# A prompt chunk's end rearranged: the second norm and two query blocks by tiles of 128 tokens, eight expert names ranked ahead of the other eight

## The reference, cut to what matters

```python
h2 = modulate(rmsnorm(x1, g_norm2), sh2, sc2)          # xn * (1 + sc2) + sh2
x2 = x1 + gt2 * peer(h2, w_pq, sub_keys, u_tab, v_tab)

def peer(h, w_pq, sub_keys, u_tab, v_tab):             # 8 heads, 128 keys a side, 16384 experts
    q = (hf @ w_pq).reshape(n, 8, 2, 128)
    s = einsum('nhsd,hskd->nhsk', q, sub_keys)
    sv, si = top_k(s, 16)                              # 16 best keys of each half
    cand = sv[:, :, 0, :, None] + sv[:, :, 1, None, :] # 256 sums
    cidx = si[:, :, 0, :, None] * 128 + si[:, :, 1, None, :]
    fv, fp = top_k(cand, 16)                           # 16 of 256 sums: 16 experts
    eidx, g = take(cidx, fp), softmax(fv)
    u, vr = u_tab[eidx], v_tab[eidx]                   # one row of 1024 numbers per token and expert
    return sum((g * gelu(h . u)) * vr)
```

## Time and profile before

| what | value |
|---|---|
| median of 3 runs | 1992.36 us (1988.22 to 1995.3) |
| the profiled execution | 1991.84 us, span 1989.4 us |
| PE busy | 1354.3 us (68%) |
| DVE busy | 1252.0 us (63%) |
| POOL busy | 1094.6 us (55%) |
| ACT busy | 589.5 us (30%) |
| DMA | 701.83 MB, mean 353 GB/s; 545.33 MB of them by the gathers |
| first gather of `u_tab` starts at | 382.5 us |

### The profile page before, as it was taken

How to read it: one execution, slowest core, us unless ns; L and a number is a source line. 1 busy time by engine, 2 the same in 40 slices (tenths; PEclk the granted TensorE clock), 3 DMA queues, 4 the chain that set the end, 5 groups by cost and what they waited for, 6 DMA issues and landing times.

```text
span 1989.4 us, 23567 instructions
## 1 busy us (share of the span) xinstructions
PE 1354.3 (68%) x7318; PEld 873.8 (44%) x7318; DVE 1252.0 (63%) x3037; ACT 589.5 (30%) x1653; POOL 1094.6 (55%) x1062
## 2 busy tenths in 40 slices
PE   6998999857879677988878777444443444544344
PEld 5887799745646445666655544111110111111111
DVE  3265436477788888866667756656667666666640
ACT  2446424233245245222223323112112212211110
POOL 0100000256665556765666767777777777677774
PEclk9999999978989889889989888556566666765667
DMA  9755346699999988999999999999999999999997
GB/s 366 261 176 206 108 159 200 217 382 370 396 349 407 343 324 328 385 409 370 408 407 409 409 407 396 400 409 404 403 407 401 408 403 402 381 409 408 390 402 292
DMA packets 202443, 701.83 MB, mean 353 GB/s; under 512 B 22568, under 2 KB 32368, under 8 KB 202032
## 3 DMA queue, kind: packets, MB, share of 16 engines
q0 software_dynamic: 149760, 545.33, 70.0%
q1 hardware_dynamic: 52560, 155.02, 21.3%
HBM read 691.26 MB, written 11.06 MB: 353 GB/s over the span
## 4 chain that ended last, share of the span: by engine, by line
DMA 20%; issue 14%; POOL 14%; PE 8%; DVE 3%; POOLq 0%; ACT 0%; DVEq 0%; ACTq 0%
DMA arena<-in_v_tab,pku 14%; POOL arena L2153 14%; DMA arena<-in_u_tab,pku 6%; PE y L1149 5%; PE acc L796 2%; DVE arena L1990 1%; PE acc L936 1%; POOLq L2149 0%; DVE pku L2011 0%; PE acc L833 0%; DVE pk L2010 0%; PE turned L1132 0%; DVE pku L2027 0%; DVE arena L1611 0%; DVE pk L2026 0%
## 5 line engine op out<-in xcount | busy, mean ns | idle before, releaser
L1149 PE MATMUL y<-arena 128*32 128x512 f32 x2080 | 413.8, 909 | 495.9 <-DMA arena<-in_v_tab,pku 495.8
L2153 POOL DMA_INDIRECT arena<-in_u_tab,pku x520 | 551.7, 1061 | 344.9 <-issue 156.3
L2153 POOL DMA_INDIRECT arena<-in_v_tab,pku x520 | 527.9, 1015 | 294.0 <-issue 149.1
L796 PE MATMUL acc<-arena 128*128 128x264 f32 (+1 forms) x2304 | 547.4, 395 | 17.4 <-ACT arena L1259 7.8
L796 PEld LDWEIGHTS acc<-arena 128*128 128x128 f32 x2304 | 445.4, 196 | 122.5 <-issue 49.7
L1990 DVE CUSTOM_DVE_ANT_0 arena<-arena,h_bank 128x1024 f32<-128x1024 f32 x240 | 290.8, 1218 | 254.1 <-DMA arena<-in_u_tab,pku 253.3
L1149 PEld LDWEIGHTS y<-arena 128*32 128x32 f32 x2080 | 81.8, 143 | 728.2 <-issue 723.5
L1990 DVE CUSTOM_DVE_ANT_0 arena<-arena 128x1024 f32<-128x1024 f32 x280 | 335.2, 1221 | 84.7 <-DMA arena<-in_u_tab,pku 72.4
L1486 ACT ACTIVATE pk<-pk 128x1 f32<-128x1 f32 x520 | 103.5, 281 | 2.1
L1504 ACT CAST pku<-turned 128x8 uint32<-128x8 f32 x64 | 10.3, 160 | 293.6 <-PE turned L1133 293.6
L1132 PE MATMUL turned<-arena 128*128 128x256 f32 x128 | 58.2, 545 | 55.5 <-DVE arena L2068 55.4
(11 more groups left out here) (249 smaller groups left out, 1873.5 us busy)
## 6 DMA issues: line engine op xcount, KB each, us to landing
arena<-w_mod SPq DMA_DIRECT2D x48, 512.0 KB, 6.2
arena<-w_pq SPq DMA_DIRECT2D x32, 512.0 KB, 7.1
arena<-w_xr SPq DMA_DIRECT2D x20, 512.0 KB, 9.0
arena<-w_qk SPq DMA_DIRECT2D x20, 512.0 KB, 7.0
arena<-w_gr SPq DMA_DIRECT2D x20, 512.0 KB, 6.5
arena<-w_rnn SPq DMA_DIRECT2D x16, 640.0 KB, 7.1
arena<-in_u_tab,pku POOLq DMA_INDIRECT x520, 8.0
arena<-in_v_tab,pku POOLq DMA_INDIRECT x520, 7.8
```

Of the source, the lines that this page charges most:

```text
L796: mm = pe.matmul(a[:, 0:n], w[:, k, :], rhs[:, k, 0:n], start=(k == 0), stop=(k == ks - 1))
L1149: mm = pe.matmul(y[rows, h, :], spread[g % NTURN][:, 32 * j:32 * j + 32], rows_v[j][:, h * 512:(h + 1) * 512], start=first and (g != SAMPL ...
L2153: pool.indirect_dma_start(out=row, out_offset=None, in_=table, in_offset=bass.IndirectOffsetOnAxis(ap=idx, axis=0), **more).then_inc(signa ...
```

## The change

The products of chunk 0 behind `norm` 1 are put in another order and two of them are cut in half. Behind the norm come `pqa` 0 and 1 (query blocks 0 and 1 for the first 128 tokens), `first`, `pqb` 0 and 1 (the same blocks for the other 128 tokens), then `mod` 10, `mod` 11, `modT` 10, `modT` 11, then `rowsx` 0 to 3, then `pq` 2 and on as before. h2 is made tile by tile: DVE multiplies by the gain (`scale_tiles`), ACT adds the shift (`shift_rows`). A new function `first_names` on DVE finds the eight best names of head 0 from the 64 sums of the 8 best keys of each side and writes them itself; POOL's first gather waits for it (`s_first`). The other eight names come as before, from 16 keys of each side and 256 sums, out of `best_keys`, `best_sums`, `experts` and `number`. ACT runs `spread_keys`, the copies up to `rowsx` 2, `number` and `exponentials` in this order. The weights of `pq` 0, `pq` 1 and `keys` 0 take the ring's places ahead of those of `mod` 10 and 11, and `pq` 2 and 3 are loaded when `pqb` 0 and 1 are done.

```diff
+        "gains": [("mod", 10), ("mod", 11), ("modT", 10), ("modT", 11)]}
...
         product(ch, "norm", 1, (), 3.5)
-        mods(ch, "norm")
+        if ch == 0:
+            for c in range(2):
+                product(0, "pqa", c, (("pq", c),), 1.8)
+            product(0, "first", 0, (("keys", 0),), 0.5)
+            for c in range(2):
+                product(0, "pqb", c, (("pq", c),), 0.3)
+            mods(0, "gains")
         for i in range(2 * (CT + ch)):
-            product(ch, "rowsx", i, (), 1.0)
-        mods(ch, "rows")
+            product(ch, "rowsx", i, (), 1.0 if ch else 0.3)
...
+            def shift_rows(t, cs):
+                for c in cs:
+                    act.wait_ge(s_scaled, DC * t + c + 1)
+                    rows = h2T[:, c, t * P:(t + 1) * P]
+                    act.activation(rows, rows, ACT.Identity, bias=mod[:, 3 * DC + c, 0:1]).then_inc(s_hb if t else s_h, 1)
...
             course.until(PEER_FROM)
+            course.until(NO[0, "pqb", 1] + 1)
             spread_keys(0)
+            course.until(NO[0, "rowsx", 2] + 1)
+            number(0)
             exponentials(0)
-            number(0)
...
+            def scale_tiles():
+                await_read(dve, 0, "norm", 1)
+                for t in range(CT):
+                    cols = slice(t * P, (t + 1) * P)
+                    link(dve.reciprocal(rstd2[:, cols], rstd2[:, cols]))
+                    for c in range(DC):
+                        dve.scalar_tensor_tensor(h2T[:, c, cols], x1[:, c, cols], mod[:, 4 * DC + c, 0:1], rstd2[:, cols],
+                                                 ALU.mult, ALU.mult).then_inc(s_scaled, 1)
...
+            def first_names():
+                await_read(dve, 0, "first", 0)
+                for half in range(2):
+                    x, b = stage[0][:, half * NKEYS:(half + 1) * NKEYS], best[:, half, 0:SLOT]
+                    rank(dve.max(b, x))
+                    rank(dve.max_index(keyi[:, 16 * half:16 * half + SLOT], b, x))
...
+                few = cand[:, 0:SLOT * SLOT]
...
+                rank(dve.max(fv[:, 0:SLOT], few))
+                rank(dve.max_index(posi[:, 0:SLOT], fv[:, 0:SLOT], few))
...
+                dve.scalar_tensor_tensor(eidx[0][:, 0:SLOT], pickq[:, 0:SLOT], float(NKEYS), pickq[:, SLOT:2 * SLOT],
+                                         ALU.mult, ALU.add).then_inc(s_first, 1)
...
             course.until(PEER_FROM)
+            first_names()
             best_keys(0)
...
+                    elif g == 0:
+                        pool.wait_ge(s_first, 1)
```

More of the change, by code:

```diff
@@ L118, in mods @@
         for what, i in MODS.get(place, ()) if ch == 0 else ():
-            product(0, what, i, tuple(("mod", 4 * i + q) for q in range(4)) if what == "mod" else (), 4.0 if what == "mod" else 0.5)
+            product(0, what, i, tuple(("mod", 4 * i + q) for q in range(4)) if what == "mod" else (), (0.5 if place == "gains" else 4.0) if what == "mod" else 0.2)
     def block(ch, name, c):
@@ L225, in _slots @@
     for p in PIECES:
-        late = int(FIRST[p] >= PEER_FROM)
-        if p == (0, "keys", 0):
-            place[1] = place[0] % (OWN + EXTRA) + 1
+        late = int(FIRST[p] >= NO[0, "rowsx", 0])
+        if not late:
+            place[1] = (place[0] + 1) % (OWN + EXTRA)
         s = place[late] % (OWN if late else OWN + EXTRA)
@@ L965, in key_products @@
                 for c in range(4 * pair, 4 * pair + 4):
-                    await_read(pe, ch, "pq", c)
+                    if ch == 0 and c < 2:
+                        await_read(pe, 0, "pqa", c)
+                        await_read(pe, 0, "pqb", c)
+                    else:
+                        await_read(pe, ch, "pq", c)
                 for t in range(CT + ch):
@@ L1075, in chunk @@
                     square_sum(ch, 1, squares2)
-                yield from modulations(ch, "norm")
+                if ch == 0:
+                    for c in range(2):
+                        yield NO[0, "pqa", c]
+                        project_tile("pqa", c, 0)
+                    yield from first_scores()
+                    for c in range(2):
+                        yield NO[0, "pqb", c]
+                        project_tile("pqb", c, 1)
+                    yield from modulations(0, "gains")
                 yield from token_rows(ch, "rowsx", x1)
-                yield from modulations(ch, "rows")
                 for pair in range(PH // 2):
-                    for c in range(4 * pair, 4 * pair + 4):
+                    for c in range(4 * pair if ch or pair else 2, 4 * pair + 4):
                         yield NO[ch, "pq", c]
                         project(ch, "pq", c, h2T)
-                        if ch == 0 and c == 1:
-                            yield from first_scores()
                     yield NO[ch, "keys", (CT + ch) * pair]
@@ L1390, in chunk @@
                 root(ch, 1)
-                yield from modulations(ch, "norm")
+                if ch == 0:
+                    shift_rows(0, range(DC))
+                    yield NO[0, "pqa", 0]
+                    query_tile("pqa", 0, 0)
+                    shift_rows(1, range(4))
+                    yield NO[0, "pqa", 1]
+                    query_tile("pqa", 1, 0)
+                    yield NO[0, "first", 0]
+                    a = take(0, "first", 0)
+                    release(act.copy(stage[0], a[:, 0:2 * NKEYS]), 0, "first", 0)
+                    shift_rows(1, range(4, DC))
+                    for c in range(2):
+                        yield NO[0, "pqb", c]
+                        query_tile("pqb", c, 1)
+                    yield from modulations(0, "gains")
                 for i in range(2 * (CT + ch)):
```

82 lines of the change are left out of this document (54 added, 28 removed).

## The result

The changed kernel's median is 2000.73 us (seven runs, 1995.73 to 2003.97) against 1991.11 of the kernel before beside it: a ratio of 1.0046, 95% interval 1.0033 to 1.0060. A second measurement, twelve runs beside other runs of the kernel before, gave 1999.56 against 1992.29, 1.0032 (1.0019 to 1.0044). So by these ratios the change costs 6 to 9 us. That is inside the predicted range of 1984 to 2002, at its upper part, but outside the forecast's own of 1988 to 1998. It is on the slower side of the bound of 0.3%, which had a chance of 0.21 and which the second interval still includes; the forecast had "the same" at 0.57.

What follows compares the result with a forecast made beforehand. The prediction took the gathers on the DMA engines to bound the kernel: +0.1 at head 1's names and +0.9 up to head 2 make +1.0 us on 1991.84, so 1993 us, range 1984 to 2002 (8 in 10).

Steps and rivals of the forecast that it cites:

- the forecast's own: The narrower range of the main forecast alone, without the rivals: 1988 to 1998 us.
- the bound of 0.3%: What a measurement of this kernel can tell from no change, 6 us; slower by more had chance 0.21.
- "the same": The outcome that the changed kernel's time stays within 0.3% of the kernel before, chance 0.57.
- The first chain: From the norm to head 0's names and POOL's first gather: it starts at 370.1, 12.4 us earlier.
- The second chain: From the norm through `pq` 2, 3, `keys`, `rowsh` and dots to head 1's names: seventeenth gather moves +0.1 us.
- a new hole: Nine early gathers fill the old hole; another opens at 383 to 395 while POOL waits for the first dot.
- Up to head 2: `LIMITS` shifts by one or two products, chunk 1's first norm comes later: net +0.9 us; other gather-loop work moves along.
- The prediction's own sign of being wrong: Seventeenth gather more than 3 us off, or the stages from 425 to 820 losing or winning over 4 us themselves.
- the allowance: Small shifts of dense work against the quarters up to 820 us can add or take 4 us.
- The slower one, head 1's scores late: Head 1's scores, stored at 391, land at 408 and cost 7 us: 1999 us, chance 0.2.
- the head start arrives in full: First gather 12.4 us earlier and everything follows: 1980 us, decided by a first dot before about 385, chance 0.07.

Runs made afterwards that it cites:

- e4: The changed kernel with POOL's first gather made to wait for `number` as well, as before the change: 1996.90 us, ratio 1.0023.
- e11: The kernel before with the changed kernel's `MIDDLE` and `LIMITS` from quarter 12 on, nothing else: 1997.93 us, ratio 1.0033.
- e1: The changed kernel with zero costs for the new products ahead of `pq` 2, so the plan's tables are those of before: 1999.93 us, ratio 1.0038.
- e5: e1 with `pq` 2, 3, `keys` 0, 1 and `rowsh` directly behind `pqb`, `mod` 10, 11 and `rowsx` behind them: 1988.96 us, ratio 0.9985.
- e7: e5 with head 1's scores copied on the chip by ACT instead of through DRAM: 1989.16 us, ratio 0.9983.
- e12: e7 with the four `rowsx` left where the changed kernel has them: 1985.61 us, ratio 0.9971.
- e8: e1 with head 1's scores copied on the chip by ACT instead of through DRAM: 1993.95 us, ratio 1.0003.
- e2: The kernel before with `pq` 2's cost raised from 3.6 to 6.8, giving the changed kernel's tables from quarter 4 on: 1994.84 us, ratio 1.0020.

## Why the prediction was right, and where it failed

**The first chain** was right in sum, with two sizes off. The root ended 0.65 earlier in this execution. Then `pqa` 0 and 1 took 5.70 and ended at 364.64, where the working gives 363.1 - 0.65 = 362.5: no slow stretch had been counted there. PE had been idle for 2.54 us before them, and the clock fell 1.4 us after it had begun again. Windows of 1 us of the changed kernel show the granted clock:

```profile
359.00:360.00 1.00, 1.00 (x8) 1.00 (x8) 1.00 (x5) 1.00 (x5) 0.00 (x0) 1.00 1.02 359
...
361.00:362.00 1.00, 1.00 (x7) 1.00 (x7) 0.96 (x5) 0.00 (x0) 0.00 (x0) 0.50 0.79 277
...
364.00:365.00 1.00, 0.87 (x8) 0.68 (x7) 0.00 (x0) 0.27 (x1) 0.00 (x0) 1.00 0.00 0
```

By windows of 0.2 us it is 0.50, which is 1.2 GHz, from about 360.3 to 363.7. Copy, `first` and copy took 1.3 for 1.9, `first_names` 4.15 (365.93 to 370.08) for 4.1, and the first gather came at 371.0 for 370.1, inside the bounds. Eight passes over 128 columns took 2.19, 0.274 each, between the 0.25 chosen and the estimated 0.29 of the Trainium skill (VectorE: DVE Perf Modes, the section on the errata of SBUF-source operations); that each instruction pays a fixed part, as the page says, this trace bears out: one `tensor_tensor` of 64 columns takes 0.224 us (L2075), one of 128 columns 0.291 to 0.292 (L2083, L2086). The passes of the row take 0.347 each by themselves, so eight in 2.19 us overlap.

**The second chain** was right: `number` at 377.57 for 376.7, the reciprocal of `shares` at 379.61, a gap of 5.21 for 5, `pq` 2 and 3 in 8.54 for 8.64, first dot at 394.19 for 394.2, ranking at 401.07 for 401.3, seventeenth gather at 415.58 for 415.8. That the first dot came within 0.01 us is in part luck: `pq` 3 ended at 389.78 for 388.8, and from `keys` to the first dot it took 3.75 (390.44 to 394.19) for 4.9, so two errors of 1 us cancelled. Two small sums of the working are off, and nothing hangs on them: 376.7 + 1.9 is 378.6 and not 378.8, and 3 less 2.4 is 0.6 and not 0.9. That a head start of 11.5 us ends in a new hole was right, and e4 shows that it is worth nothing by itself.

**The step that failed** is in "Up to head 2": "All other work in the gather loop is the same in number and length, and it moves along." Its first part, +1.0 at head 2's names, measured +1.7 and +1.5, within its bounds. The rest was put at 0 and measured +4.3 and +5.8 from the fortieth gather to the last. The working had named the cause, `LIMITS` shifting by one or two products, and allowed it 4 us of either sign; it sized it by its effect up to head 2 and not on the quarters 12 to 79 that have the same shift. e11 puts that at 0.33%, 6.6 us, in the kernel before. The prediction's own sign of being wrong, that the stages from 425 to 820 lose more than 4 us by themselves, came out in both executions: from the seventeenth gather to the 240th the distance grew from -0.1 to +5.4 and from -0.3 to +8.1. That the time still lies in the range is owed to the allowance and to the rivals that opened it, not to the sum.

How a shift of one or two products costs that much is only read, not shown. By `_limits` the tables name a product one or two places back in most quarters from 12 to about 60; between 60 and 80 they fall together, and behind that they differ in few. So the swing to 10 us ahead comes while the shift stays, and the net loss, from the 220th gather on (quarters 67 to 77), comes where it is caught up. There POOL's wait before the 230th gather is longer by 3.5 us in the changed kernel than in the one before, and it is the longest of POOL's waits in that stretch. That this wait makes the net loss is not shown; no run takes it away alone.

**The rivals.** The slower one, head 1's scores late, is a real mechanism with about the price given (6.69 us in e1, 8.34 in e5), but not in this kernel: the same shift of the plan that loses time later put the load ahead of the weights. The time of that rival, 1999, came by another road. That the head start arrives in full was to be decided by a first dot before about 385: e5 and e7, with first dots at 383.18 and 380.51, gained 3 us, and e12, with 386.24, 6, where the rival had 12, so the price was too high. Behind the dots stood head 1's scores in e5 and its `keyx` in e7.

## What to carry to other kernels

When work moves across the border from which a static plan shares out products, compare the plan's tables before and after for every later step, not for the first few; work that lies under a wait anyway can be given no cost, so that the tables stay: e8 and e12 do that, and e8 has the time of before. Set one and the same transfer of two traces side by side, at five or six places: here a flat distance came from the start, and a distance that swings from the plan. An experiment that undoes one loss and brings in another of its size, as e1 did, looks like one without effect, so read its trace before dropping the theory.

## What the runs showed of the hardware

In these runs a small load came later with what SP had issued ahead of it. The 128 KB of head 1's scores, by the view of DMA issues from 380 to 412 us (KB each, median us from issue to landing), in the changed kernel and then in e1:

```profile
arena<-key_rows SPq DMA_DIRECT2D x1, 128.0 KB, 2.3
```

```profile
arena<-key_rows SPq DMA_DIRECT2D x1, 128.0 KB, 11.7
```

Ahead of it in e1 SP had issued four loads of 512 KB and one of 256, and the gathers ran beside them; in the changed kernel nothing stood directly ahead of it, and it landed when the gathers were only starting again. A pair with gathers on both sides is the kernel before and e2, which differ in the plan alone: 11.4 us behind two loads of `w_pq` and one of `w_keys`, and 4.5 with none directly ahead. The Trainium skill (DMA: Bandwidth & Descriptors, the section on queues, rings and completion order) says that on each DMA engine descriptors are consumed in ring order; the landings agree with that. How long a load waits by size is not shown: the 11.4 stands behind fewer bytes than the 11.7.
